# Second attention of a two-layer step kernel: decode scores and product with V ahead of the second prompt step's scores in each slot

## What is computed

```python
def stick_breaking_attention(q, k, v, q_pos0):
    Tq, Tk = q.shape[1], k.shape[1]
    scale = DH_B ** -0.5
    for start in range(0, Tq, Q_BLOCK):
        stop = min(start + Q_BLOCK, Tq)
        k_end = max(1, min(Tk, q_pos0 + stop - 1))
        qb, kb, vb = q[:, start:stop], k[:, :k_end], v[:, :k_end]
        z = jnp.einsum('bqhd,bkhd->bhqk', qb, kb).astype(jnp.float32) * scale
        q_pos = q_pos0 + jnp.arange(start, stop)
        mask = jnp.arange(k_end)[None, :] < q_pos[:, None]
        log_1m = jnp.where(mask, jax.nn.log_sigmoid(-z), 0.0)
        suffix = lax.cumsum(log_1m, axis=3, reverse=True) - log_1m
        a = jnp.where(mask, jnp.exp(jax.nn.log_sigmoid(z) + suffix), 0.0)
        outs.append(jnp.einsum('bhqk,bkhd->bqhd', a.astype(v.dtype), vb))
    return jnp.concatenate(outs, axis=1)
```

## Time and profile before

| | us |
|---|---|
| median of three runs | 1642.45 |
| the runs | 1639.75, 1643.95, 1642.45 |
| the profiled execution | 1639.72 |
| its span, first to last instruction | 1637.9 |

### The profile page before, as it was taken

The page is one execution under the profiler, slowest core; times in us unless marked ns, Lnnn a source line. Parts: engine busy times, 40 slices in busy tenths (PEclk is TensorE's granted clock), DMA queues, the critical chain, the costliest instruction groups (busy, mean ns, idle before and its releaser), DMA issues.

```text
span 1637.9 us, 31443 instructions
## 1 busy us (share of the span) xinstructions
PE 1616.6 (99%) x13180; PEld 1486.7 (91%) x13180; DVE 1132.0 (69%) x1576; ACT 722.5 (44%) x1196; POOL 151.9 (9%) x132
## 2 busy tenths in 40 slices
PE   9999999999999999999999999999999999999999
PEld 8888766699999999999999897766999999999999
DVE  5765477678984797488742337877689748964874
ACT  6444476765551344134432214666555413531441
POOL 0000000012210011011000100000122101110110
PEclk9999999999999999999999999999999999999999
DMA  7133899931222122222243458997422221221222
GB/s 288 64 113 139 348 420 419 419 151 52 87 95 104 52 78 103 78 69 87 103 150 136 168 210 350 419 419 325 167 78 78 104 78 55 101 104 52 78 104 90
DMA packets 40252, 267.54 MB, mean 163 GB/s; under 512 B 4400, under 2 KB 4784, under 8 KB 10928
## 3 DMA queue, kind: packets, MB, share of 16 engines
q1 hardware_dynamic: 36720, 252.95, 40.2%
q0 software_dynamic: 3392, 12.58, 2.2%
HBM read 249.79 MB, written 15.73 MB: 162 GB/s over the span
## 4 chain that ended last, share of the span: by engine, by line
PE 86%; DMA 5%; DVE 5%; issue 2%; ACT 2%; SPq 0%; DVEq 0%; ACTq 0%
PE ps L584 30%; PE ps L799 29%; PE ps L268 4%; PE ps L270 4%; PE ps L269 4%; DMA kv<-in_v_s 3%; PE ps L1264 2%; PE ps L1323 2%; DVE s_lo L748 2%; PE ps L1205 2%; PE ps L611 2%; PE ps L1242 1%; DMA kv<-in_v_a 1%; DMA xT<-in_v_a 1%; PE ps L1227 1%
## 5 line engine op out<-in xcount | busy, mean ns | idle before, releaser
L230 ACT ACTIVATE w_hi<-w_raw 128x2048 fp32r<-128x2048 f32 x55 | 105.0, 1909 | 189.8 <-PE ps L584 158.5
L246 DVE TENSOR_TENSOR w_lo<-w_raw,w_hi 128x2048 fp32r<-128x2048 f32 x55 | 126.0, 2292 | 71.7 <-ACT w_hi L230 71.7
L744 ACT ACTIVATE s_hi<-t 128x512 fp32r<-128x512 f32 x176 | 109.4, 626 | 144.5 <-PE ps L799 65.5
L799 PE MATMUL ps<-hs_hi,s_hi 128*128 128x320 f32 x528 | 163.8, 310 | 0.0
L799 PE MATMUL ps<-hs_lo,s_hi 128*128 128x320 f32 x528 | 163.2, 309 | 0.0
L799 PE MATMUL ps<-hs_hi,s_lo 128*128 128x320 f32 x528 | 163.2, 309 | 0.0
L584 PE MATMUL ps<-gu_hi,w_hi 128*128 128x320 f32 x692 | 157.8, 309 | 0.2
L584 PE MATMUL ps<-gu_lo,w_hi 128*128 128x320 f32 x692 | 157.7, 309 | 0.0
L584 PE MATMUL ps<-gu_hi,w_lo 128*128 128x320 f32 x692 | 157.7, 309 | 0.0
L748 DVE TENSOR_TENSOR s_lo<-t,s_hi 128x512 fp32r<-128x512 f32 x176 | 133.0, 762 | 5.3 <-ACT s_hi L744 4.5
L657 DVE TENSOR_TENSOR sg<-ps,rows 128x640 f32<-128x640 f32 x47 | 38.7, 823 | 128.5 <-PE ps L584 128.5
(11 more groups left out here) (302 smaller groups left out, 3968.2 us busy)
## 6 DMA issues: line engine op xcount, KB each, us to landing
w_raw<-in_w SPq DMA_DIRECT2D x99, 1024.0 KB, 4.8
kv<-in_k_a SPq DMA_DIRECT2D x12, 1024.0 KB, 17.7
kv<-in_v_a SPq DMA_DIRECT2D x12, 1024.0 KB, 18.0
kv<-in_v_s SPq DMA_DIRECT2D x12, 1024.0 KB, 17.0
kv<-in_k_s SPq DMA_DIRECT2D x12, 1024.0 KB, 20.3
xT<-in_k_a SPq DMA_DIRECT2D x8, 1024.0 KB, 18.6
xT<-in_k_s SPq DMA_DIRECT2D x8, 1024.0 KB, 13.7
work<-in_v_a SPq DMA_DIRECT2D x7, 1024.0 KB, 16.5
```

What stands on the lines that cost most here:

```text
L230: nc.scalar.activation(w_hi[s][:, :, :], w_raw[:, s, :, :], ACT.Copy).then_inc(hi_done, 1)
L246: nc.vector.tensor_tensor(w_lo[s][:, :, :], w_raw[:, s, :, :], w_hi[s][:, :, :].bitcast(F32), ALU.subtract).then_inc(lo_done, 1)
L744: nc.scalar.activation(s_hi[i][:, :, :], factor(j % 2, i), ACT.Copy).then_inc(hi_done, 1)
L799: last = nc.tensor.matmul(ps[:, bank[i], 0:HALF], w[:, p, :], m[:, p, :], start=(i < 3 and p == 0 and a == 0), stop=(p == 3 and a == 2), s ...
```

## The change

In every slot but the last, the decode scores of piece n+1 and the product with V of piece n now come ahead of the scores of prompt step k+2 on TensorE; on ScalarE the decode sigmoids come ahead of the sigmoid of step k+2, and on VectorE the decode scan and multiply ahead of the scans of step k+2. No instruction changes otherwise.

```diff
@@ pe_b
                     if n + 1 < N_PAIRS:
-                        self.pe_ps(k + 2)
                         self.pe_s(n + 1)
                         self.pe_v(n)
+                        self.pe_ps(k + 2)
                     if n > 0:
                         self.pe_pv(k - 1)
@@ act_b
-                    if k + 2 < STEPS:
-                        self.act_pu(k + 2)
                     if n >= N_PAIRS - 5:
                         self.act_hi(n - (N_PAIRS - 5))
                     if n + 1 < N_PAIRS:
                         self.act_sx(n + 1)
-                    else:
+                    if k + 2 < STEPS:
+                        self.act_pu(k + 2)
+                    if n + 1 == N_PAIRS:
                         act.wait_ge(*self.last_used("w_hi0"))
                         split_hi(act, first, 0, 0)
@@ dve_b
                     if n % 2 == 0 and n + 2 < N_PAIRS:
                         self.dve_q(n // 2 + 1)
+                    if n + 1 < N_PAIRS:
+                        self.dve_sprod(ch, n + 1)
                     if k + 2 < STEPS:
                         self.dve_prod(ch, k + 2)
-                    if n + 1 < N_PAIRS:
-                        self.dve_sprod(ch, n + 1)
```

## The result

The changed kernel takes 1646.53 us (median of 15 runs, 1645.16 to 1653.43) against 1641.67 us of the kernel before in the same comparison (15 runs, 1639.69 to 1643.95): a ratio of 1.0033, interval 1.0024 to 1.0042. It is 4.9 us slower; 3.0 us were forecast. The profiled execution took 1648.26 us.

The account below looks back on a forecast made before the run. TensorE, busy 99% of the span, was taken as the bound, nearly level with the load stream in the second attention; 6.5 - 2.1 - 1.4 = +3.0 us on 1642.45 gave 1645.4 us, range 1642 to 1649.5.

Parts of the forecast that it names:

- the prompt sigmoid is hidden: Even slots: ScalarE's prompt sigmoid ends 0.11 us before TensorE needs its banks, behind the product with prompt V.
- load waits vanish: Slots 10, 13 and 14: TensorE's load waits of 0.15, 1.56 and 0.42 us go as it comes later, 2.1 us.
- Rival A: Second attention's end: the load of slot 14 still decides, so only +1.65 us; chance 0.22.
- Rival C: Second attention: faster, through earlier freed ring places and earlier w1, at best -2 us; chance 0.04.
- The term for TensorE alone: Second attention: new TensorE waits, 1.3 us in slot 0 plus 7 x 0.75 us in slots 2 to 14, 6.5 us.
- The even slot's price: Even slots: TensorE waits 0.75 us for VectorE's late prompt scan before the transposes of step k+2.
- the odd slots: Odd slots: no wait, and a gain of at most some 0.05 us, left out of the sum.
- Slot 0: First slot, with no product with prompt V: w1 starts at 1005.88 instead of 1004.60, +1.3 us.
- The holes: Slots 6 and 10: TensorE's issue holes of 0.72 and 1.40 us stay in place, hiding 1.4 us of new wait.
- rival B: Slower: thin sigmoid cover fails, holes hide nothing or VectorE's chain is longer; +4.4 to +6.5 us; chance 0.15.
- rival D: The clock falls: one slot at the lower clock level doubles its 9.3 us, +9.3 us; chance 0.01.

Follow-up runs that it names:

- cut loads: Second attention's cached K and V loads after the first ten cut to half their columns: kernel before 1634.22 us, changed kernel 1642.37 us.
- changed, scans cut: Changed kernel with cut loads, the two product scans of the moved 384-key prompt step also cut to 128 columns: 1638.44 us.
- odd slots only: Kernel before with the changed order in odd slots only, old order in even ones: 1650.66 us; with cut loads 1636.89 us.
- even-slots kernel: Kernel before with the changed order in even slots only (384-key prompt step moved), old order in odd ones: 1645.27 us, ratio 1.0021.
- four in flight, odd slots: Kernel before with changed order in odd slots only and at most four second-attention cached K and V loads in flight from the eleventh: 1652.18 us.

## Why the prediction was right, and where it was not

**Right: the place and the kind of the loss.** VectorE's scan of the moved 384-key step ends behind the point where TensorE wants its transposes; the wait shows in slots 0, 2 ... 14, odd slots have no such wait, the prompt sigmoid is hidden by 0.10 us (0.11 said), load waits vanish, VectorE is idle for 2.18 us ahead of the decode scan (about 2 said), and the output projection starts late (1157.44 in the profiled execution, about 1152 said). Rival A did not come: TensorE does not wait for V in slot 14. Rival C did not either.

**The term for TensorE alone was too small.** Summed at 6.5 us, it measures 8.15 us with the cut loads. Its parts can be read from one w1 to the next, here over slots 2 and 3 of the profiled executions with cut loads:

| kernel | w1 of slot 2 at | to w1 of slot 3 | to w1 of slot 4 |
|---|---|---|---|
| before | 1013.28 | 9.73 | 8.76 |
| changed | 1015.34 | 10.57 | 8.90 |
| changed, scans cut | 1014.88 | 9.81 | 9.19 |
| odd slots only | 1013.86 | 9.73 | 9.22 |

The even slot's price was right: 10.57 - 9.73 = 0.84 us against 0.75, and 0.08 without the scan, so the scan it is. What failed is that I costed the odd slots at nothing. Alone they cost 9.22 - 8.76 = 0.46 us here and 2.7 us in all, because of what the prompt scores had hidden: they stood between the end of the transposes and the decode scores, and covered VectorE's `dve_o` and ScalarE's copies, on which the decode scores wait. In the full change TensorE's delay in the even slot gives `dve_o` time, and only 0.14 us stay; with the scans cut it is 0.43 again. So the 3.9 us that cutting the scans gave is a lower bound for their price. Slot 0 was 1.7 us instead of 1.3; of that, 0.34 us is a wait for a copy. Together, 1.7 + 7 x 0.8 + 0.6 in the odd slots + about 0.5 for the hole of 0.38 us is 8.4 us, against 8.45 in the stage. With the loads as they are, a pair of slots grew to 1044.95 - 1025.43 = 19.52 us, by 0.97 instead of 0.75.

**The holes did not do what the term said.** I took them to stand still and to hide 1.4 us. In the profiled executions the one of slot 6 (0.72) is gone, that of slot 10 grew from 1.40 to 1.80 and took the place of a wait for the scan, and slot 13 got a new one of 1.87 us, where the load wait of 1.56 us had been; the sum went from 2.5 to 4.1 us, with 1.6 us more at a lower clock (from 1135.30 to 1139.63 for what took 2.71 us before). In the medians it looks otherwise: the loads as they are cost the kernel before 1641.64 - 1634.22 = 7.4 us and the changed one 1646.53 - 1642.37 = 4.2 us. Of the 3.3 us between them 2.1 (by the profiled executions) are the load waits that went, which was forecast; some 1.1 us are left for holes and clock together. That is near the 1.4 us of the forecast by luck, for the holes moved and grew instead of hiding a wait.

**Near in sum, partly for wrong reasons.** 8.15 - 3.3 = 4.9 us is 1.9 more than forecast and inside the range; 1.65 us of the miss is the order's term, and the odd slots are the largest part that it left out. Of rival B only the part came by which the holes hide little; a wait for the prompt sigmoid beyond slot 0, its other part, did not.

The clock fell for short stretches, at a far smaller price (1.6 us in the profiled execution) than the 9.3 us that rival D put on it. The Trainium skill, "Perfetto Trace Analysis", section Matmul Optimizations, says that the matmul engine scales its power with utilization, so that matmuls should run back to back. These traces agree in part: the granted clock stayed at 1.00 at the regular waits of 0.5 us, and fell behind some holes of 1.66 us and more.

**Open.** Why TensorE's packet starts about 3 us after the boundary at some points of the grid and 6 to 7 us at others beside a full stream, no run here settles; nor why the odd-slots order meets 6.86 us at slot 3, where the kernel before has 3.11 and the full change 2.81. The lengths repeat (a hole of 2.77 us in two kernels), so chance of the moment alone it is not.

## What to carry to other kernels

Before moving an instruction, list what it covers where it stands: here short prompt scores hid copies and a small evacuation that two engines owed to the matmul behind them, and uncovering those cost 2.7 us in the odd slots alone, where the forecast had nothing. A wait is not gone when another engine's work is taken forward; ask what that engine now does later. And where a stage runs with full transfer queues, judge a small reordering with the loads thinned out as well: the 8.2 us between the orders were clear there, while the loads as they are added 7.4 us to one order and 4.2 to the other.

## What was not expected of the hardware

TensorE's instructions come in packets of about 16.4 KB, some 124.5 matmul records each, and beside a load stream of 419 GB/s the engine can stand idle at such a boundary until 1.25 to 1.60 us after the packet has landed: 0.2 to 2.8 us at a time, up to 9.6 us in a stage of 165 us. With cut loads (235 GB/s in the window shown) it was 0 to 0.4 us in the whole stage. Bounding the loads in flight to four changed nothing in it.

Behind holes of 1.80 us (even-slots kernel, slot 10) and 1.87 us (changed kernel, slot 13) the windows shown above have a granted clock of 0.66 and 0.67, a mix of the two levels (2.4 and 1.2 GHz), and from the end of one of 1.66 us (four in flight, odd slots, 1075.41 to 1079.41) it was 0.62; from the end of one of 1.80 us in slot 10 of the changed kernel (1102.63 to 1106.63) it stayed at 1.00.
